# Keeping four w1 chunks and two query chunks in four slots of the gather ring, in a two-layer decoder trunk on one Trainium2 core

## The chip, the core and the metric

The kernel runs on one core of one Trainium2 chip. The metric is the time on the device in microseconds, from the start of the program to its end; the median of several runs counts, and lower is better. A difference of 0.2% (3.2 us here) is about the smallest that this measurement can tell from no change.

## What is computed

A trunk of two layers over 256 tokens of width 1024, in float32. Layer 0 mixes sparse attention with retention, layer 1 is a gated convolution module, and each is followed by a PEER step, in which every token picks 128 rows (8 heads, 16 picks each) out of 16384 experts and needs their `u` and `v` rows in full:

```python
q = (xf @ w_q).reshape(T, P_HEADS, 2, P_QDIM // 2)
...
eidx = (e1 * P_NKEYS + e2).reshape(T, P_HEADS * P_TOPK)
...
hb = jnp.einsum('td,tkd->tk', xb, u[ib])
act = jax.nn.gelu(hb, approximate=False) * gb
return jnp.einsum('tk,tkd->td', act, v[ib])
...
a = h @ w_pw1 + b_pw1                      # conformer module of layer 1
a = a[..., :D] * jax.nn.sigmoid(a[..., D:])
```

## The kernel before

The tokens are two tiles of 128, one token to a partition. The PEER work is four passes `p`: layer 0 tile 0, layer 0 tile 1, layer 1 tile 0, layer 1 tile 1. A pass has 8 rounds `i` of 16 picks, so there are 512 picks, numbered here n = 128p + 16i + r. One pick is one indirect gather by POOL (L441) of 8 KB for each of 128 partitions (`u` and `v` of one expert for each token), 1.05 MB, into one slot of `ring`, which has 16 slots. DVE takes the dot product of the `u` half with the token (L984), ACT turns four dots into gelu times gate and four diagonal matrices (L596 to L605), and PE multiplies those with the `v` half into PSUM (L1430), pick by pick in pairs, and counts each on the semaphore `v_multiplied`. A slot is free when its pick is multiplied. `AHEAD = 5` is the number of gathers that may be under way: gather n waits until gather n-5 has landed.

Everything else stands between these picks, in an order written out by hand. DVE has its top-k of the next queries (`heads_step`), the 31 taps of the convolution (`conv_taps`), norms and sums between dots, at fixed rounds and picks. PE has after each batch of four picks what `first_beside`, `beside` and `conv_beside` say: the query products (L1181 into `side`), the products with `w1` (`conv_in`, L1181 into `pm`) and `w2` (`conv_out`), and the scores (L1402). The convolution of tile 0 runs in pass 1, that of tile 1 in pass 2; `conv_in` stands at the (round, batch) pairs `CONV_INS = [(0, 2), (0, 3), (1, 1), (1, 2), (1, 3), (2, 0), (2, 1), (2, 2)]`. The queries of heads 6 and 7 of passes 2 and 3 are multiplied in round 1 of these passes, after batch 0.

The weights come in chunks of 1 MB through a buffer of two, `wbuf`, in the order of `CHUNKS`, issued by SP (L352); a chunk is loaded when PE has multiplied the one two places before it. The 8 chunks of `w1` are loaded once for each tile; query chunks 6 and 7 of layer 1 are loaded once for pass 2 and once for pass 3. Gathers and weights run on the same 16 DMA engines.

Of the kernel before, what the change touches and what calls it, by code (L numbers as in the profile page):

```python
# [7 lines left out]
D = 1024  # L8
KD = D // P
# [9 lines left out]
P_HEADS, P_TOP = 8, 16  # L19
# [16 lines left out]
RING = 16  # L36
# [20 lines left out]
X_OF_NORM = [0, 0, 1, 2, 3, 4, 5, 6, 7, 8]  # L57

def weight_chunks():

    order = [("o", 0, c) for c in range(4)] + [("q", 0, h) for h in range(4)]
    order += [("o", 1, c) for c in range(4)] + [("q", 0, h) for h in range(4, 8)] + [("q", 1, h) for h in range(4)]
    for p in (1, 2):
        order += [("w1", p - 1, c) for c in range(2)]
        if p == 2:
            order += [("q", 2, 6), ("q", 2, 7)]
        order += [("w1", p - 1, c) for c in range(2, KD)] + [("w2", p - 1, c) for c in range(4)]
        order += [("q", p + 1, h) for h in range(6)]
    return order + [("q", 3, 6), ("q", 3, 7)]


CHUNKS = weight_chunks()
SELECTIONS = [(0, 0), (0, 1), (0, 2), (1, 2), (0, 3), (1, 3), (1, 0), (1, 1)] + [(p, i) for p in (2, 3) for i in range(4)]


# [15 lines left out]
def hybrid_decoder_trunk_kernel(nc, x, gains, w_in, kv_norm, uk_t, uv_w, w_o, rot, decay,  # L91
# [9 lines left out]
    with ctx:  # L101
# [159 lines left out]
        lead_ready, gate_exp = sem("lead_ready"), sem("gate_exp")  # L261
        gathered = [sem(f"gathered{r}") for r in range(RING)]
        idx_copied, may_gather = sem("idx_copied"), sem("may_gather")
        picks_ready = [sem(f"picks_ready{t}") for t in range(TILES)]
# [44 lines left out]
        def _(sp):  # L309
# [24 lines left out]
            def multiplied(n):  # L334
# [6 lines left out]
                return (wo_ps if kind == "o" else w2_ps), p * 4 + c + 1  # L341

            def load_chunks(kind, p, first, end):

                view = {"o": w_o, "q": wq_l[p // 2], "w1": w1, "w2": w2}[kind]
                for c in range(first, end):
                    n = CHUNKS.index((kind, p, c))
                    if n >= WBUF:
                        sp.wait_ge(*multiplied(n - WBUF))
                    else:  # L350
                        sp.wait_ge(ret_s_ready, 1)
                    sp.dma_start(wbuf[:, n % WBUF, :, :].rearrange("p k c -> p (k c)"), view[:, c, :]) \  # L352
                      .then_inc(w_loaded[n % WBUF], 16)
# [12 lines left out]
            load_gain("bias", 0)  # L366
            load_chunks("w1", 0, 0, KD)
            load_gain("norm", 5)
# [20 lines left out]
        def _(pool):  # L389
# [23 lines left out]

            def gathers(p, first, pairs):

                layer, t = p // 2, p % 2
                rounds = PICKS // RING
                with pool.Fori(0, pairs) as i:
                    for half in range(2):
                        r0 = p * rounds + first + half  # L420
                        if p != 1:
                            pool.wait_ge(picks_ready[t], i * 2 + (layer * rounds + half + 1))
                        pool.wait_ge(v_multiplied, i * (2 * RING) + (r0 * RING + 1))
                        pool.sem_inc(may_gather, 1)
                        pool.tensor_copy(idx_now[:, half, :], eidx[:, t, ds(i * (2 * RING) + (first + half) * RING, RING)]) \  # L425
                            .then_inc(idx_copied, 1)
                        pool.wait_ge(idx_copied, i * 2 + (r0 + 1))
                        for r in range(RING):
                            freed = r0 * RING + r + 1
                            pool.wait_ge(v_multiplied, i * (2 * RING) + freed)  # L430
                            if r0 == 0 and r in in_use:
                                if in_use[r]:
                                    pool.wait_ge(proj_ps, job_of(*in_use[r]) + 1)
                                else:
                                    pool.wait_ge(b_t_ready, 2)
                            if r >= AHEAD:
                                pool.wait_ge(gathered[r - AHEAD], i * 32 + 16 * (r0 + 1))
                            elif p or half:
                                pool.wait_ge(gathered[r - AHEAD + RING], i * 32 + 16 * r0)
                            pool.sem_inc(may_gather, 1)  # L440
                            pool.indirect_dma_start(ring[:, r, :], None, table[layer],  # L441
                                                    bass.IndirectOffsetOnAxis(idx_now[:, half, r:r + 1], 0)) \
                                .then_inc(gathered[r], 16)

            pool.wait_ge(a_ready, 2)
            gathers(0, 0, 4)
            pool.wait_ge(picks_ready[1], P_HEADS - 2)
            gathers(1, 0, 1)
            pool.wait_ge(picks_ready[1], P_HEADS)
            gathers(1, 2, 3)  # L450
            gathers(2, 0, 4)
            gathers(3, 0, 4)

# [263 lines left out]
        def _(dve):  # L717
# [256 lines left out]
            def expert_round(p, i, between=None):  # L974


                t = p % 2
                rounds = PICKS // RING

                for r in range(RING):  # L980
                    if between:
                        between(r)
                    dve.wait_ge(gathered[r], i * 16 + 16 * (p * rounds + 1))
                    dve.scalar_tensor_tensor(out=ring[:, r, 0:D], in0=ring[:, r, 0:D], scalar=1.0, in1=h_tok[:, t, :],  # L984
                                             op0=ALU.mult, op1=ALU.mult, accum_out=hb[:, r:r + 1]).then_inc(dots_ready, 1)
# [183 lines left out]
        def _(pe):  # L1169
# [245 lines left out]
            def expert_round(p, i, between=None):  # L1415
# [4 lines left out]
                for b, (first, end) in enumerate(batches(p, i)):  # L1420
                    for r0 in range(first, end, 2):
                        pair = range(r0, min(r0 + 2, end))
                        pe.wait_ge(diag_ready, p * PICKS + i * RING + pair[-1] + 1)
                        for c in range(2):
                            for r in pair:
                                odd = r % 2 if (p, i) != LAST or r < RING - 1 else 0
                                for half in range(2):
                                    rows = slice(half * HALF, (half + 1) * HALF)
                                    j = (half + odd) % 2
                                    step = pe.matmul(acc[odd][c][j * HALF:(j + 1) * HALF, :], diag[rows, r % (2 * BATCH), :],  # L1430
                                                     ring[rows, r, D + c * COLS:D + (c + 1) * COLS],
                                                     start=(i == 0 and r0 == 0), stop=(i == 7 and r == last_pick[odd]))
# [172 lines left out]
```

## Time and profile before

| | |
|---|---|
| median of 3 runs | 1593.21 us (1592.16 to 1594.64) |
| the profiled execution | 1591.96 us, span of its instructions 1590.2 us |
| mean granted TensorE clock | 0.819 |
| busy over the span | PE 1020.0 us, DVE 1096.9 us, ACT 462.7 us, POOL 678.4 us |
| moved by DMA | 622.17 MB, mean 391 GB/s |

Busy time is a sum over stages with different limits, so it says little by itself: what matters is what each engine waits for in a stretch. The span falls into the mixer of layer 0 (to some 137 us, where the first gather is issued), pass 0, pass 1 (picks 128 to 255), pass 2 (256 to 383) and pass 3 (384 to 511).

### The profile page before, as it was taken

The page shows a single profiled execution, that of the slowest core. Times are in us where ns is not written, and L with a number is a line of the kernel's source. Part 1 is how long each engine was busy: PE and PEld are TensorE (multiplying, and loading weights), DVE is VectorE, ACT ScalarE, POOL GpSimd, SP SyncE. Part 2 cuts the span into 40 slices and gives each one's busy share as a digit, 9 for nine tenths or more (in the row PEclk, how much of TensorE's full clock was granted, in tenths as well). Part 3 has the DMA queues.
Part 4 walks back from the last instruction along what each step waited for, and adds up shares of the span by engine and source line. Part 5 has one row for each costly group of instructions (what it writes and reads, how often), then busy time and mean ns, then how long its engine had stood idle before and what let it go on. Part 6 is the DMA issues. An engine that isn't in the chain of part 4 may idle for free.

```text
span 1590.2 us, 20959 instructions
## 1 busy us (share of the span) xinstructions
PE 1020.0 (64%) x6998; PEld 536.9 (34%) x6998; DVE 1096.9 (69%) x2839; ACT 462.7 (29%) x1442; POOL 678.4 (43%) x566
## 2 busy tenths in 40 slices
PE   7999747555566586566745667546675557555565
PEld 7796424222333143223413335312332223111111
DVE  2745565887777877985457789899558777744445
ACT  2221313322223433333313333324142223322223
POOL 0002434443444445674334345465333435554552
PEclk9999878677777897878878879967987778787768
DMA  9046999999999999999999999999999999999996
GB/s 381 25 167 256 368 421 420 419 421 402 407 420 421 399 422 420 421 420 421 421 421 421 420 420 416 419 385 414 421 421 420 421 415 412 418 421 420 416 421 275
DMA packets 86883, 622.17 MB, mean 391 GB/s; under 512 B 9600, under 2 KB 10368, under 8 KB 12800
## 3 DMA queue, kind: packets, MB, share of 16 engines
q0 software_dynamic: 73728, 536.90, 81.7%
q1 hardware_dynamic: 12912, 83.74, 13.0%
q8 instruction: 55, 0.90, 0.2%
q14 instruction: 44, 0.36, 0.1%
q10 hardware_dynamic: 144, 0.26, 0.0%
HBM read 619.82 MB, written 1.05 MB: 390 GB/s over the span
## 4 chain that ended last, share of the span: by engine, by line
DMA 62%; PE 22%; DVE 11%; ACT 2%; issue 1%; DVEq 1%; ACTq 0%; POOL 0%; POOLq 0%
DMA ring<-experts_dram,idx_now 61%; PE side L1430 7%; PE pm L1181 7%; DVE ring L984 5%; PE side L1181 4%; ACT act_v L599 1%; DMA wbuf<-w_dram 1%; ACT diag_all L605 1%; DVE top_i L904 1%; DVE top_i L920 0%; DVE onehot L905 0%; PE side L1402 0%; DVE best_i L929 0%; DVE diag_all L932 0%; DVE best_i L940 0%
## 5 line engine op out<-in xcount | busy, mean ns | idle before, releaser
L441 POOL DMA_INDIRECT ring<-experts_dram,idx_now x512 | 659.4, 1288 | 734.4 <-DMA ring<-experts_dram,idx_now 398.2
L1430 PE MATMUL side<-ring,diag_all 64*64 64x512 f32 x2056 | 627.3, 766 | 537.6 <-ACT diag_all L605 537.6
L984 DVE SCALAR_TENSOR_TENSOR ring<-ring,h_tok 128x1024 f32<-128x1024 f32 x512 | 607.5, 1222 | 158.4 <-DMA ring<-experts_dram,idx_now 151.8
L1430 PE MATMUL pm<-ring,diag_all 64*64 64x512 f32 x2040 | 623.2, 766 | 0.0
L1430 PEld LDWEIGHTS side<-ring,diag_all 64*64 64x64 f32 x2056 | 172.7, 173 | 938.2 <-ACT diag_all L605 575.0
L596 ACT ACTIVATE ge<-hb 128x4 f32<-128x4 f32 (+1 forms) x130 | 26.7, 206 | 864.5 <-DVE ring L984 864.3
L1430 PEld LDWEIGHTS pm<-ring,diag_all 64*64 64x64 f32 x2040 | 170.6, 173 | 0.0
L605 ACT ACTIVATE diag_all<-ident,act_v 128x64 f32<-128x64 f32 x512 | 136.6, 336 | 10.6
L1053 DVE SCALAR_TENSOR_TENSOR conv_buf<-conv_buf,chan_sb 128x128 f32<-128x128 f32 x480 | 128.6, 340 | 0.0
L599 ACT ACTIVATE act_v<-ge,gates 128x1 f32<-128x1 f32 x512 | 109.2, 283 | 9.5 <-issue 0.7
L901 DVE MAX8 top_v<-side 128x8 f32<-128x128 f32 x64 | 15.2, 289 | 116.7 <-PE side L1402 116.6
L1181 PEld LDWEIGHTS side<-h_t,wbuf 128*128 128x128 f32 x768 | 87.0, 192 | 10.1 <-issue 9.4
L1181 PE MATMUL side<-h_t,wbuf 128*128 128x128 f32 x768 | 89.4, 277 | 0.5 <-DMA wbuf<-wq_dram 0.5
L1181 PEld LDWEIGHTS pm<-hc_t,wbuf 128*128 128x128 f32 x512 | 58.4, 192 | 13.4 <-issue 11.7
L1181 PE MATMUL pm<-hc_t,wbuf 128*128 128x128 f32 x512 | 61.3, 278 | 0.9 <-DMA wbuf<-w_dram 0.9
L425 POOL COPY idx_now<-eidx 128x16 uint32 (+1 forms) x32 | 12.4, 388 | 99.9 <-ACT conv_buf L547 73.3
L1181 PE MATMUL pm<-conv_buf,ring 128*128 128x128 f32 x448 | 53.7, 280 | 0.2 <-DVE ring L831 0.2
L596 ACT ACT_TABLE_LOAD x41 | 52.6, 1283 | 1.6
L1181 PEld LDWEIGHTS pm<-conv_buf,ring 128*128 128x128 f32 x448 | 52.3, 194 | 1.4 <-DVE ring L831 0.6
L984 DVE DVE_READ_ACCUMULATOR ring<-ring,h_tok 128x1 f32 x512 | 41.3, 81 | 0.0
L1181 PE MATMUL pm<-ring,conv_buf 128*128 128x512 f32 (+2 forms) x128 | 35.3, 429 | 1.1 <-ACT conv_buf L469 1.1
L1181 PE MATMUL pm<-wbuf,hc_t 128*128 128x256 f32 x128 | 30.6, 398 | 6.3 <-DMA wbuf<-w_dram 6.3
(200 smaller groups left out, 830.7 us busy)
## 6 DMA issues: line engine op xcount, KB each, us to landing
wbuf<-wq_dram SPq DMA_DIRECT2D x28, 1024.0 KB, 11.0
wbuf<-w_dram SPq DMA_DIRECT2D x24, 1024.0 KB, 9.8
ring<-w_in_dram SPq DMA_DIRECT2D x5, 2048.0 KB, 22.2
wbuf<-w_o_dram SPq DMA_DIRECT2D x8, 1024.0 KB, 7.9
ring<-experts_dram,idx_now POOLq DMA_INDIRECT x512, 11.7
gain<-gains_dram SPq DMA_DIRECT2D x7, 512.0 KB, 13.0
ring<-w_in_dram SPq DMA_DIRECT2D x1, 1696.0 KB, 9.7
x_tok<-x_dram SPq DMA_DIRECT2D x2, 512.0 KB, 4.8
```

The lines of the kernel that those rows point to most:

```text
L425: pool.tensor_copy(idx_now[:, half, :], eidx[:, t, ds(i * (2 * RING) + (first + half) * RING, RING)]) \
L441: pool.indirect_dma_start(ring[:, r, :], None, table[layer], bass.IndirectOffsetOnAxis(idx_now[:, half, r:r + 1], 0)) \
L596: act.activation(ge[:, first:end], hb[:, first:end], ACT.Gelu)
L599: last = act.activation(act_v[:, r:r + 1], ge[:, r:r + 1], ACT.Copy, scale=gates[:, t, i * RING + r:i * RING + r + 1])
L605: act.activation(diag[:, r % (2 * BATCH), :], ident2[:, :], ACT.Copy, scale=act_v[:, r:r + 1]).then_inc(diag_ready, 1)
L901: dve.max(top_v[:, b, j, 0:8], side[b, j])
L904: dve.max_index(top_i[:, b, j, 0:8], top_v[:, b, j, 0:8], side[b, j])
L984: dve.scalar_tensor_tensor(out=ring[:, r, 0:D], in0=ring[:, r, 0:D], scalar=1.0, in1=h_tok[:, t, :], op0=ALU.mult, op1=ALU.mult, accum_out ...
L1053: step = dve.scalar_tensor_tensor(out=dst, in0=src, scalar=tap, in1=dst, op0=ALU.mult, op1=ALU.add)
L1181: last = pe.matmul(dst, lhs(k), rhs(k), start=(k == 0), stop=(k == KD - 1))
L1430: step = pe.matmul(acc[odd][c][j * HALF:(j + 1) * HALF, :], diag[rows, r % (2 * BATCH), :], ring[rows, r, D + c * COLS:D + (c + 1) * COLS] ...
```

## The change

Ring slots 12 to 15 hold weights for a time. When tile 0's last picks of layer 0 (124 to 127) are multiplied, chunks 0 to 3 of `w1` are loaded into these four slots, and both tiles' convolutions read them there. When tile 1's `conv_in` is through with chunks 0 and 1, query chunks 6 and 7 of layer 1 go into slots 12 and 13 and serve passes 2 and 3. In all, six loads of 1 MB fall away. Slots 14 and 15 are given back to the gathers at pick 296, slots 12 and 13 at pick 416. So the gathers have 12 slots for picks 128 to 295, 14 for 296 to 415, and 16 otherwise. A pick takes the free slot that was used longest ago, by a table `SLOTS` made when the program is built; POOL's gathers, in loops with a register before, are written out one by one.

```diff
+KEPT = 4
+KEPT_IN = {("w1", c): RING - KEPT + c for c in range(KEPT)} | {("q", 6): RING - KEPT, ("q", 7): RING - KEPT + 1}
+KEPT_FROM = PICKS
+KEPT_TO = {RING - KEPT + c: 3 * PICKS + 2 * RING if c < 2 else 2 * PICKS + 2 * RING + 8 for c in range(KEPT)}
...
+def pick_slots():
+    last, uses, slots = {r: r - RING for r in range(RING)}, {r: 0 for r in range(RING)}, []
+    for n in range(4 * PICKS):
+        free = [r for r in range(RING) if r not in KEPT_TO or not KEPT_FROM <= n < KEPT_TO[r]]
+        r = min(free, key=lambda r: last[r])
+        uses[r] += 1
+        slots.append((r, uses[r], max(last[r], n - RING)))
+        last[r] = n
+    return slots
...
+            def load_kept(kind, p, c):
+                r = KEPT_IN[(kind, c)]
+                if kind == "w1":
+                    sp.wait_ge(v_multiplied, RING + max(n for n in range(KEPT_FROM) if SLOTS[n][0] == r) + 1)
+                else:
+                    sp.wait_ge(pw_ps, KD + r - RING + KEPT + 1)
+                view = {"q": wq_l[p // 2], "w1": w1}[kind]
+                sp.dma_start(ring[:, r, :], view[:, c, :]).then_inc(kept_loaded[r - RING + KEPT], 16)
...
-            load_chunks("w1", 0, 0, KD)
+            for c in range(KEPT):
+                load_kept("w1", 0, c)
+            load_chunks("w1", 0, KEPT, KD)
...
-            load_chunks("w1", 1, 0, 2)
-            load_chunks("q", 2, 6, 8)
-            load_chunks("w1", 1, 2, KD)
+            for c in (6, 7):
+                load_kept("q", 2, c)
+            load_chunks("w1", 1, KEPT, KD)
...
-            load_chunks("q", 3, 2, 8)
+            load_chunks("q", 3, 2, 6)
...
+                    for n in range(n0, n0 + RING):
+                        r, use, freed = SLOTS[n]
+                        if freed >= 0:
+                            pool.wait_ge(v_multiplied, RING + freed + 1)
...
+                        if n >= AHEAD:
+                            pool.wait_ge(gathered[SLOTS[n - AHEAD][0]], 16 * SLOTS[n - AHEAD][1])
                         pool.sem_inc(may_gather, 1)
+                        pool.indirect_dma_start(ring[:, r, :], None, table[layer],
+                                                bass.IndirectOffsetOnAxis(idx_now[:, i % 2, n - n0:n - n0 + 1], 0)) \
+                            .then_inc(gathered[r], 16)
...
             def chunk(kind, p, c):
+                if (kind, c) in KEPT_IN and (kind == "w1" or p > 1):
+                    r = KEPT_IN[(kind, c)]
+                    pe.wait_ge(kept_loaded[r - RING + KEPT], 32 if kind == "q" else 16)
+                    return ring[:, r, :].rearrange("p (k c) -> p k c", k=KD)
```

SP's queue around the start of pass 1, before the change: the bias row and the eight `w1` chunks of tile 0, two at a time through `wbuf` (line 332 loads a row of gains or biases, line 352 a weight chunk; the wait named is the semaphore of what must be multiplied first):

```order
L332 DMA gain<-b_dram 128x1024 [waits h_ready]
L352 DMA wbuf<-w_dram 128x2048 [waits q_ps] x2
L352 DMA wbuf<-w_dram 128x2048 [waits pw_ps] x6
L332 DMA gain<-gains_dram 128x1024 [waits h_ready]
L352 DMA wbuf<-w_dram 128x2048 [waits pw_ps] x2
```

The same place after the change (line 351 loads a row, 370 a chunk into the ring, 381 a chunk into `wbuf`):

```order
L351 DMA gain<-b_dram 128x1024 [waits h_ready]
L370 DMA ring<-w_dram 128x2048 [waits v_multiplied] x4
L381 DMA wbuf<-w_dram 128x2048 [waits q_ps] x2
L381 DMA wbuf<-w_dram 128x2048 [waits pw_ps] x2
L351 DMA gain<-gains_dram 128x1024 [waits h_ready]
L381 DMA wbuf<-w_dram 128x2048 [waits pw_ps] x2
L381 DMA wbuf<-w_dram 128x2048 [waits w2_ps] x2
```

Four chunks now wait for multiplied picks, and chunks 4 and 5 stand right behind them in one queue, with a wait that is long over.

POOL's queue at the boundary between rounds 0 and 1 of pass 1, picks 142 to 147, before the change (the copy sets the indices of the next round; `gatheredN` is the landing of the gather into slot N, here that of pick n-5):

```order
L441 DMA ring<-experts_dram,idx_now 128x2048 [waits v_multiplied,gathered9]
L441 DMA ring<-experts_dram,idx_now 128x2048 [waits v_multiplied,gathered10]
L425 COPY idx_now<-eidx 128x16 [waits v_multiplied]
L441 DMA ring<-experts_dram,idx_now 128x2048 [waits gathered11,idx_copied,v_multiplied]
L441 DMA ring<-experts_dram,idx_now 128x2048 [waits v_multiplied,gathered12]
L441 DMA ring<-experts_dram,idx_now 128x2048 [waits v_multiplied,gathered13]
L441 DMA ring<-experts_dram,idx_now 128x2048 [waits v_multiplied,gathered14]
```

The same seven places after the change:

```order
L472 DMA ring<-experts_dram,idx_now 128x2048 [waits v_multiplied,gathered9]
L472 DMA ring<-experts_dram,idx_now 128x2048 [waits v_multiplied,gathered10]
L455 COPY idx_now<-eidx 128x16 [waits v_multiplied]
L472 DMA ring<-experts_dram,idx_now 128x2048 [waits gathered11,idx_copied,v_multiplied]
L472 DMA ring<-experts_dram,idx_now 128x2048 [waits v_multiplied,gathered0]
L472 DMA ring<-experts_dram,idx_now 128x2048 [waits v_multiplied,gathered1]
L472 DMA ring<-experts_dram,idx_now 128x2048 [waits v_multiplied,gathered2]
```

After slot 11 comes slot 0, and 12 to 15 are left out. The order of gathers, dots and products is the same; what moved is the slot that each uses, and with it the multiplied pick that POOL waits for: from pick 140 on n-12, in place of n-16.

## Rows read from the trace of the kernel before

**Rows 1.** Page, part 2: DMA share and rate in 40 slices.

```profile
DMA  9046999999999999999999999999999999999996
GB/s 381 25 167 256 368 421 420 419 421 402 407 420 421 399 422 420 421 420 421 421 421 421 420 420 416 419 385 414 421 421 420 421 415 412 418 421 420 416 421 275
```

**Rows 2.** Page, parts 3 and 6: queues; issues (count, KB, us to landing).

```profile
q0 software_dynamic: 73728, 536.90, 81.7%
q1 hardware_dynamic: 12912, 83.74, 13.0%
...
wbuf<-w_dram SPq DMA_DIRECT2D x24, 1024.0 KB, 9.8
...
ring<-experts_dram,idx_now POOLq DMA_INDIRECT x512, 11.7
```

**Rows 3.** Windows: PE, PEld, DVE, ACT, POOL busy; clock, DMA share, GB/s.

```profile
490.00:810.00 320.00, 201.10 (x1406) 100.44 (x1409) 233.86 (x583) 107.17 (x318) 163.86 (x118) 0.83 1.01 418
810.00:1331.00 521.00, 319.75 (x2231) 161.63 (x2224) 404.81 (x1127) 161.92 (x498) 235.65 (x192) 0.81 1.01 416
1331.00:1580.00 249.00, 148.52 (x911) 47.50 (x912) 137.51 (x269) 58.92 (x241) 120.42 (x101) 0.77 0.99 412
```

**Rows 4.** DVE's waits for gathers in 490:810, 810:1331, 1331:1580 (us, times, longest).

```profile
DVE ring L984 <- DMA ring<-experts_dram,idx_now: 31.3, 23, 3.7
...
DVE ring L984 <- DMA ring<-experts_dram,idx_now: 8.2, 7, 1.6
...
DVE ring L984 <- DMA ring<-experts_dram,idx_now: 108.6, 87, 2.2
```

**Rows 5.** Timeline around 1180: DVE's last gather wait, its next wait; PE.

```profile
1183.16 1.22 DVE L984 SCALAR_TENSOR_TENSOR ring<-ring,h_tok 128x1024 f32<-128x1024 f32 x1 [1.23 <-DMA ring<-experts_dram,idx_now]
...
1193.52 0.94 DVE L901 MAX8 top_v<-side 128x8 f32<-128x128 f32 x4 [9.12 <-PE side L1402]
...
1178.29 7.41 PE L1181 MATMUL side<-h_t,wbuf 128*128 128x128 f32 x64
```

**Rows 6.** The gathers' line: time from issue to landing, min, median, max.

```profile
DMA to landing us min/median/max: 5.7/11.7/20.3
```

**Rows 7.** Timeline of SP: issues of weight chunks that fall away or move.

```profile
490.24 3.90 SPq L352 DMA_DIRECT2D wbuf<-w_dram  x2
...
896.08 3.90 SPq L352 DMA_DIRECT2D wbuf<-w_dram  x2
...
1271.77 3.90 SPq L352 DMA_DIRECT2D wbuf<-wq_dram  x2
```

**Rows 8.** Pass 1: PE ends 128; POOL's 140, copy, 144; DVE's dot 147.

```profile
541.27 1.06 PE L1430 MATMUL pm<-ring,diag_all 64*64 64x512 f32 x2
...
529.94 0.94 POOL L441 DMA_INDIRECT ring<-experts_dram,idx_now  x1 [2.94 <-DMA ring<-experts_dram,idx_now]
...
542.50 0.78 POOL L425 COPY idx_now<-eidx 128x16 uint32<-128x16 uint32 x1 [5.02 <-PE pm L1430]
544.11 1.09 POOL L441 DMA_INDIRECT ring<-experts_dram,idx_now  x1 [0.83 <-PE pm L1430]
...
564.25 1.22 DVE L984 SCALAR_TENSOR_TENSOR ring<-ring,h_tok 128x1024 f32<-128x1024 f32 x1
...
569.49 0.35 DVE L1038 SCALAR_TENSOR_TENSOR conv_buf<-pm,chan_sb,gate_sig 128x128 f32<-128x128 f32 x1 [2.87 <-ACT gate_sig L616]
```

**Rows 9.** Before pick 200: PE finishing 184, 185; DVE's dot 200.

```profile
694.00 1.06 PE L1430 MATMUL pm<-ring,diag_all 64*64 64x512 f32 x2
...
713.01 1.22 DVE L984 SCALAR_TENSOR_TENSOR ring<-ring,h_tok 128x1024 f32<-128x1024 f32 x1 [0.42 <-DMA ring<-experts_dram,idx_now]
```

**Rows 10.** Pick 412: PE ends 396; POOL's gather 410; DVE's dot 412.

```profile
1317.99 1.06 PE L1430 MATMUL pm<-ring,diag_all 64*64 64x512 f32 x2
...
1314.68 1.89 POOL L441 DMA_INDIRECT ring<-experts_dram,idx_now  x1 [1.70 <-issue]
...
1331.60 1.22 DVE L984 SCALAR_TENSOR_TENSOR ring<-ring,h_tok 128x1024 f32<-128x1024 f32 x1 [0.19 <-DMA ring<-experts_dram,idx_now]
```

More of the change, by code:

```diff
@@ L262, in hybrid_decoder_trunk_kernel @@
         gathered = [sem(f"gathered{r}") for r in range(RING)]
+        kept_loaded = [sem(f"kept_loaded{c}") for c in range(KEPT)]
         idx_copied, may_gather = sem("idx_copied"), sem("may_gather")
@@ L412, in _, with gathers @@
                                        base=P * t, pattern=[[-1, s]], channel_multiplier=1).then_inc(done, 1)
-            def gathers(p, first, pairs):
+            def gathers(p, first, end):
                 layer, t = p // 2, p % 2
[L417 to L423, printed above, removed]
-                        pool.sem_inc(may_gather, 1)
[L425 to L443, printed above, removed]
@@ new lines, in gathers @@
+                for i in range(first, end):
+                    n0 = p * PICKS + i * RING
+                    if p != 1:
+                        pool.wait_ge(picks_ready[t], layer * P_HEADS + i + 1)
+                    if n0:
+                        pool.wait_ge(v_multiplied, n0 + 1)
+                    pool.sem_inc(may_gather, 1)
+                    pool.tensor_copy(idx_now[:, i % 2, :], eidx[:, t, i * RING:(i + 1) * RING]).then_inc(idx_copied, 1)
+                    pool.wait_ge(idx_copied, n0 // RING + 1)
+                    for n in range(n0, n0 + RING):
+                        r, use, freed = SLOTS[n]
+                        if freed >= 0:
+                            pool.wait_ge(v_multiplied, RING + freed + 1)
+                        if n < RING and r in in_use:
+                            if in_use[r]:
+                                pool.wait_ge(proj_ps, job_of(*in_use[r]) + 1)
+                            else:
+                                pool.wait_ge(b_t_ready, 2)
+                        if r >= RING - KEPT and n >= KEPT_TO[r] and all(SLOTS[m][0] != r for m in range(KEPT_TO[r], n)):
+                            c = r - RING + KEPT
+                            pool.wait_ge(*((q_ps, nth_head(3, 3, c)) if c < 2 else (pw_ps, KD + c + 1)))
+                        if n >= AHEAD:
+                            pool.wait_ge(gathered[SLOTS[n - AHEAD][0]], 16 * SLOTS[n - AHEAD][1])
+                        pool.sem_inc(may_gather, 1)
+                        pool.indirect_dma_start(ring[:, r, :], None, table[layer],
+                                                bass.IndirectOffsetOnAxis(idx_now[:, i % 2, n - n0:n - n0 + 1], 0)) \
+                            .then_inc(gathered[r], 16)
@@ L445, in _ @@
             pool.wait_ge(a_ready, 2)
[L446 removed]
+            gathers(0, 0, 8)
             pool.wait_ge(picks_ready[1], P_HEADS - 2)
[L448 removed]
+            gathers(1, 0, 2)
             pool.wait_ge(picks_ready[1], P_HEADS)
[L450 to L452 removed]
+            gathers(1, 2, 8)
+            gathers(2, 0, 8)
+            gathers(3, 0, 8)
         @block.scalar
@@ L982, in expert_round @@
                         between(r)
-                    dve.wait_ge(gathered[r], i * 16 + 16 * (p * rounds + 1))
-                    dve.scalar_tensor_tensor(out=ring[:, r, 0:D], in0=ring[:, r, 0:D], scalar=1.0, in1=h_tok[:, t, :],
+                    slot, use, _ = SLOTS[p * PICKS + i * RING + r]
+                    dve.wait_ge(gathered[slot], 16 * use)
+                    dve.scalar_tensor_tensor(out=ring[:, slot, 0:D], in0=ring[:, slot, 0:D], scalar=1.0, in1=h_tok[:, t, :],
                                              op0=ALU.mult, op1=ALU.mult, accum_out=hb[:, r:r + 1]).then_inc(dots_ready, 1)
```

12 lines of the change are left out of this document (5 added, 7 removed).

## The prediction

> **What bounds the kernel now.** I number picks n = 128p + 16i + r. I first read the rate of the DMA engines: from slice 6 on it stands at 400 to 421 GB/s with few dips, also in the windows 490 to 810 us and 810 to 1331 us, where it moves 418 and 416 GB/s [rows 1, 3]. The gathers are 81.7% of the engines' span and SP's weights 13.0% [rows 2]. By that view the kernel is bound by transfers, and each byte less is time gained. The second view says otherwise for one stretch: how long DVE, the first user of each gather, waited for gathers. From 490 to 810 us it waited 31.3 us in 23 waits, from 1331 us to the end 108.6 us in 87, which is every pick; but from 810 to 1331 us only 8.2 us in 7 waits [rows 4]. In these 521 us (picks 233 to 411) DVE works off top-k steps, convolution taps and dots at its own pace, and the transfers run ahead of it into the ring. Of the 8.2 us, six waits lie between 1170 and 1184 us, and the timeline shows that they hide behind PE: right after the last of them (1.23 us) DVE waits 9.12 us for scores from PE, which had to do query products from 1178.29 to 1185.70 us before it came to these picks at all [rows 5]. So the kernel has three parts: transfers set the pace to pick 232, the chain DVE, ACT, PE from there to pick 411, and transfers again from 412 to the end.
>
> **What the fewer bytes give.** Six chunks of 1024 KB are 6.29 MB, at 421 GB/s [rows 1] 14.9 us of the DMA engines. Four of them stood at 896 us and after, two at 1271 us [rows 7]. Both places lie in the middle part, where DVE does not wait for gathers. The gathers then run further ahead, until they find no free slot; dot 411 ends where it did. What can be gained is what the transfers may be ahead of DVE when the third part begins, and the slots limit that.
>
> **Where the third part starts.** A gather needs, after the product that frees its slot, 0.83 us to its issue (the gather behind the index copy [rows 8]) and then at least 5.7 us to land, the least of all 512, with the queue nearly empty; the median is 11.7, with others ahead of it [rows 6]. With 14 slots gather 410 waits for the product of pick 396, the first behind a long DVE step. It ends at 1317.99 + 1.06 = 1319.05 us [rows 10]. Landing is 1319.05 + 0.83 + 5.7 = 1325.6 us, and pick 412, two gathers of 2.49 us later (1.049 MB at 421 GB/s), lands at 1330.6 us. Before, DVE began dot 412 on its landing, at 1331.60 us [rows 10]. So at the best 1.0 us of the 14.9 is left. (With 16 slots pick 412 itself would wait for pick 396, and 6.0 us would be left.) Between 5.7 and 11.7 us I take 7.2, near the short end, since the ring is drained then: +1.5 us. This term: -1.0 + 1.5 = +0.5 us.
>
> A rule of the Trainium skill gives another price (DMA: Bandwidth & Descriptors, Anatomy of one DMA): some 2.0 us fixed and the bytes at 436 GB/s. That is 4.4 us for a gather, an estimate from the page; the trace's least is 5.7 us. By the page the best case would be 2.3 us in place of 1.0.
>
> **What the slots cost at pass 1.** The four kept chunks wait for picks 124 to 127. Gather 140 waited for pick 124 too, before, and was issued at 529.94 us [rows 8], so they start about then, and chunks 4 and 5 follow at once: 6.29 MB, 14.9 us of all engines, to 545 us. Before, the first two were issued at 490.24 us [rows 7]. Gather 140 now needs slot 0 and so pick 128, multiplied at 541.27 + 1.06 = 542.33 us [rows 8]. It lands at 542.33 + 0.83 + 5.7 = 548.9 us, up to 1.5 us later where the loads still take half of the engines. Pick 147, seven gathers of 2.49 us on, lands at 566.3 to 567.8 us. DVE began its dot at 564.25 us [rows 8], so DVE is 2.1 to 3.6 us late; I take 3. The next wait of DVE, 2.87 us for the gate's sigmoid [rows 8], comes from ACT's work on these same dots, and moves with them. It does not absorb the delay.
>
> DVE catches up with the gathers at pick 200, which it started on landing at 713.01 us [rows 9]. With 12 slots gather 196 waits for pick 184, 694.00 + 1.06 = 695.06 us, 3 us later now: 698.1 + 0.83 + 5.7 = 704.6, and pick 200 lands at 714.6 us, 1.6 us later than before; with the 7.2 us of above, 3.1. I take 2.5. From 200 to 232 DVE mostly waits for gathers, so this passes whole to pick 232, and from there by the chain to pick 411 and to the third part, whose start was worked out from the product of pick 396.
>
> **Costs taken as nothing.** SP: the kept chunks hold the queue to 530 us; chunk 0 is needed behind the products of picks 136 to 139, and even 128's ends at 542.33 us. Without that cover PE would stand, and the gates and taps behind it. SP's waits for query chunks 6 and 7 are the ones of before, and only `w1` chunks 4 and 5 queue behind them. POOL's register steps go, 0.05 us or so a gather, and five gathers under way cover it. Pass 0 keeps its 16 slots. In pass 2 gathers come later by up to some 10 us, but there the ring lies well ahead of DVE, which waited for almost none [rows 4]. From nothing to a few us is possible here, and only as loss.
>
> **Sum.** +2.5 for the chain, +0.5 for the restart: +3.0 us on the profiled execution's 1591.96 us (span 1590.2 and 1.8 around it) is 1595.0 us. The median of the runs is 1.25 us above that execution: 1593.21 + 3.0 = **1596.2 us**, 0.19% slower, at the edge of what can be told from no change (0.2%, 3.2 us).
>
> **Rivals.** *The bytes count.* The Trainium skill says (DMA: Bandwidth & Descriptors, Issuing engines are not separate DMA queues) that transfers of all issuing engines share the same 16 DMA engines; so fewer weights would be faster gathers. The rates in rows 1 and 3 speak for it: the engines stand at 416 GB/s in the middle part too. Against it speak DVE's waits there. As a mechanism: if the gathers of the middle part let DVE and PE finish sooner, or if the engines lose less at restarts than I think, up to 14.9 us come off: 1593.2 - 14.9 = 1578.3; half, 1585.8. It decides for itself if dot 411 ends before 1326 us. I give 1578 to 1590 a chance of 0.18.
>
> *The restarts cost more.* Each time the ring is full and then drains, a landing may take the 11.7 us of the median, not 5.7 to 7.2, as gathers free in pairs and weights land beside them. Then pick 200 is 1.6 + 6.0 = 7.6 us late, and pick 412 4.5 us more than I took: 1593.2 + 7.6 - 1.0 + 6.0 = 1605.8 us. It decides from some 9 us from issue to landing. Chance 0.26, 1600 to 1606.
>
> *Mine*, 1591 to 1600: 0.56. Slots that do not bind (the change would do only what it says, and the gain would still not arrive) give 1592 and are its low end.
>
> **Numbers.** The range of 8 in 10 cuts the far half of the bytes' case and little of the other: 1586 to 1606; mine alone is 1591 to 1600. Faster by over 0.2%: 0.17, nearly all of the bytes' case. Slower by over 0.2% (above 1596.4): the second rival's 0.26 and 0.19 of mine, 0.45. Within: 0.38.
>
> **What would show it.** SP's queue at 77.4 MB. Dips under 400 GB/s at 540 to 560 us and several between 860 and 1330 us, where now there is hardly one. POOL's waits for the product line longer. Dot 200 begins at 714 to 717 us, and dot 412 2 to 5 us later than now; the 99 picks behind it take 2.5 us each as before. In the middle DVE's waits for gathers stay under 15 us. I am wrong if dot 147 is on time (the loads and gather 140 then did not collide), if the middle part gets shorter, or if gathers after a full ring land 9 us or more after issue.

## The result, and the profile after

The changed kernel takes 1598.84 us (median of 6 runs, 1596.89 to 1600.9), the kernel before 1592.79 us beside it (6 runs, 1592.16 to 1594.64). The ratio is 1.0032, 95% interval 1.0022 to 1.0043: slower by 3.5 to 6.8 us. The profiled execution of after took 1596.89 us, span 1595.2, granted clock 0.817; it is the shortest of its six, so its trace tells a little less of the loss than the medians.

The page's part 2 of after, in slices of some 40 us, as in [rows 1]:

```profile
DMA  9046999999999999999999989999999999999997
GB/s 382 18 172 237 372 421 421 421 421 407 401 420 421 398 422 421 403 369 422 421 421 396 421 325 421 420 422 412 417 405 421 421 374 394 421 421 421 421 421 304
```

Parts 3 and 6 of the page, the queues and the gathers, as in [rows 2]:

```profile
q0 software_dynamic: 73728, 536.90, 81.7%
q1 hardware_dynamic: 12048, 77.45, 12.1%
...
ring<-experts_dram,idx_now POOLq DMA_INDIRECT x512, 11.6
```

The six loads are gone (83.74 to 77.45 MB), and there are dips that were not there: 369 in the slice from some 678 us, 396 in the one from some 837 us, 325 from some 917 us, 374 and 394 from some 1276 us. The windows, with the columns of [rows 3]:

```profile
490.00:810.00 320.00, 207.73 (x1418) 102.03 (x1416) 233.92 (x583) 106.56 (x314) 158.44 (x116) 0.81 1.00 410
810.00:1331.00 521.00, 315.08 (x2192) 159.46 (x2196) 400.90 (x1121) 161.97 (x497) 240.25 (x190) 0.80 0.98 404
1331.00:1580.00 249.00, 148.50 (x920) 48.25 (x916) 141.54 (x275) 58.94 (x242) 125.60 (x105) 0.78 1.01 421
```

In the middle part 12 GB/s less are moved over 521 us, 6.3 MB: the saved bytes. DVE did not get more done there for it (400.90 us busy, 404.81 before). DVE's waits for gathers in the same three windows (us, times, longest), for [rows 4]:

```profile
DVE ring L1015 <- DMA ring<-experts_dram,idx_now: 37.3, 29, 2.8
...
DVE ring L1015 <- DMA ring<-experts_dram,idx_now: 14.8, 7, 3.7
...
DVE ring L1015 <- DMA ring<-experts_dram,idx_now: 105.9, 85, 1.4
```

Pass 1, for [rows 8], in the timeline of after: PE ends the product of pick 128; POOL issues gather 140; DVE starts the dots of picks 140, 141 and 147, each on a landing:

```profile
544.21 1.06 PE L1466 MATMUL pm<-ring,diag_all 64*64 64x512 f32 x2
...
546.10 0.94 POOL L472 DMA_INDIRECT ring<-experts_dram,idx_now  x1 [20.87 <-PE pm L1466]
...
553.23 1.23 DVE L1015 SCALAR_TENSOR_TENSOR ring<-ring,h_tok 128x1024 f32<-128x1024 f32 x1 [1.02 <-DMA ring<-experts_dram,idx_now]
555.78 1.22 DVE L1015 SCALAR_TENSOR_TENSOR ring<-ring,h_tok 128x1024 f32<-128x1024 f32 x1 [1.31 <-DMA ring<-experts_dram,idx_now]
...
572.21 1.23 DVE L1015 SCALAR_TENSOR_TENSOR ring<-ring,h_tok 128x1024 f32<-128x1024 f32 x1 [1.25 <-DMA ring<-experts_dram,idx_now]
```

POOL stands 20.87 us before gather 140. Dot 147 begins 572.21 - 564.25 = 8.0 us later than before. Further on, POOL's gather 196, DVE's dot 200, for [rows 9]:

```profile
703.74 1.51 POOL L472 DMA_INDIRECT ring<-experts_dram,idx_now  x1 [5.61 <-PE pm L1466]
...
721.19 1.22 DVE L1015 SCALAR_TENSOR_TENSOR ring<-ring,h_tok 128x1024 f32<-128x1024 f32 x1 [0.46 <-DMA ring<-experts_dram,idx_now]
```

Dot 200 is 8.2 us later. And the start of the third part, for [rows 10]: PE ends product 396; POOL issues gather 410; DVE starts dots 412 and 413:

```profile
1324.21 1.06 PE L1466 MATMUL pm<-ring,diag_all 64*64 64x512 f32 x2
...
1326.11 0.94 POOL L472 DMA_INDIRECT ring<-experts_dram,idx_now  x1 [6.90 <-PE pm L1466]
...
1337.70 1.23 DVE L1015 SCALAR_TENSOR_TENSOR ring<-ring,h_tok 128x1024 f32<-128x1024 f32 x1
1340.19 1.23 DVE L1015 SCALAR_TENSOR_TENSOR ring<-ring,h_tok 128x1024 f32<-128x1024 f32 x1 [1.26 <-DMA ring<-experts_dram,idx_now]
```

Gather 410 waits for 396 as foreseen, and dot 412 begins 1337.70 - 1331.60 = 6.1 us later. The whole line of gathers has, from issue to landing (for [rows 6]):

```profile
DMA to landing us min/median/max: 5.4/11.6/20.7
```

The wait of POOL's gathers for products grew from 86.5 us (50 waits, the longest 6.8) to 211.8 us (71 waits, the longest 20.9):

```profile
POOL ring L472 <- PE pm L1466: 211.8, 71, 20.9
```

### The profile page after: what moved, and what is told of

It is laid out like the page before. It is cut to its first block, busy times and chain, and to the rows that moved or that the text cites. A ratio compares the mean times of both kernels' runs of the same rounds, so it can differ in the third digit from the quotient of the medians.

```text
span 1595.2 us, 20346 instructions
## 1 busy us (share of the span) xinstructions
PE 1026.8 (64%) x6998; PEld 538.7 (34%) x6998; DVE 1097.8 (69%) x2839; ACT 463.1 (29%) x1442; POOL 683.1 (43%) x566
## 3 DMA queue, kind: packets, MB, share of 16 engines
q1 hardware_dynamic: 12048, 77.45, 12.1%
## 4 chain that ended last, share of the span: by engine, by line
DVE 36%; PE 29%; DMA 21%; ACT 7%; issue 3%; DVEq 2%; ACTq 1%; POOL 0%; POOLq 0%
DMA ring<-experts_dram,idx_now 20%; DVE ring L1015 15%; PE side L1466 12%; DVE conv_buf L1084 8%; PE pm L1212 7%; PE side L1212 6%; ACT diag_all L636 2%; ACT act_v L630 2%; DVE top_i L935 1%; DVE top_i L951 1%; DVE onehot L936 1%; ACT L647 1%; DVE diag_all L963 1%; DVE best_i L960 1%; DVE best_i L971 1%
## 5 line engine op out<-in xcount | busy, mean ns | idle before, releaser
L472 POOL DMA_INDIRECT ring<-experts_dram,idx_now x512 | 667.3, 1303 | 740.1 <-DMA ring<-experts_dram,idx_now 362.8
L1466 PE MATMUL side<-ring,diag_all 64*64 64x512 f32 x2056 | 634.0, 773 | 536.5 <-ACT diag_all L636 536.4
L1466 PE MATMUL pm<-ring,diag_all 64*64 64x512 f32 x2040 | 629.9, 774 | 0.0
L1212 PEld LDWEIGHTS side<-h_t,wbuf 128*128 128x128 f32 x640 | 72.5, 192 | 8.1 <-issue 8.1
L1212 PE MATMUL side<-h_t,wbuf 128*128 128x128 f32 x640 | 74.3, 276 | 0.0
L455 POOL COPY idx_now<-eidx 128x16 uint32<-128x16 uint32 x32 | 9.2, 288 | 92.5 <-ACT conv_buf L578 72.9
L1212 PEld LDWEIGHTS pm<-hc_t,wbuf 128*128 128x128 f32 x256 | 29.2, 192 | 6.8 <-issue 6.8
L1212 PEld LDWEIGHTS pm<-hc_t,ring 128*128 128x128 f32 x256 | 29.2, 192 | 5.7 <-issue 5.7
```

Source lines behind the costliest of these rows:

```text
L472: pool.indirect_dma_start(ring[:, r, :], None, table[layer], bass.IndirectOffsetOnAxis(idx_now[:, i % 2, n - n0:n - n0 + 1], 0)) \
L1212: last = pe.matmul(dst, lhs(k), rhs(k), start=(k == 0), stop=(k == KD - 1))
```

## The experiments

The table gives, for each kernel, the median, the ratio to the kernel before with its interval, and from its trace how much later than in the trace of before the dots of some picks ended (us, less is earlier). Picks 120 and before are the same work in all, so the column for 120 is the spread from one execution to another, and 147 is read against it. Each kernel has one trace, so a difference of a us or so between two rows can be such spread too.

| kernel | median us | ratio | 120 | 147 | 232 | 396 | 412 | 511 |
|---|---|---|---|---|---|---|---|---|
| after | 1598.84 | 1.0032 [1.0022, 1.0043] | 1.7 | 8.0 | 8.4 | 6.2 | 6.1 | 4.9 |
| e_unroll | 1593.33 | 0.9999 [0.999, 1.0007] | 1.5 | 1.4 | 2.6 | 2.9 | 2.8 | 1.4 |
| e_bytes | 1588.97 | 0.9974 [0.9959, 0.9988] | 3.3 | 3.3 | 2.8 | 1.5 | 1.3 | -3.5 |
| e_slots | 1605.46 | 1.0076 [1.0063, 1.0089] | 1.0 | 7.0 | 11.3 | 12.9 | 13.3 | 13.1 |
| e_two | 1589.69 | 0.9974 [0.9963, 0.9984] | 0.8 | 0.8 | 2.0 | 1.8 | 1.6 | -3.1 |
| e_late | 1599.33 | 1.0044 [1.0027, 1.0061] | 0.7 | 6.3 | 9.5 | 5.7 | 5.6 | 5.1 |
| e_two_q | 1595.51 | 1.0002 [0.9988, 1.0016] | -0.1 | -0.1 | 2.2 | 3.3 | 3.6 | 3.5 |
| e_pass1 | 1603.12 | 1.0056 [1.0043, 1.0069] | 2.8 | 7.8 | 12.4 | 10.8 | 11.0 | 11.1 |
| e_rest | 1597.96 | 1.0024 [1.0011, 1.0037] | 2.0 | 2.1 | 5.0 | 3.6 | 6.2 | 6.1 |
| e_back | 1594.09 | 0.9999 [0.999, 1.0008] | 1.9 | 6.9 | 8.0 | 5.5 | 5.3 | 3.6 |
| e_three | 1589.34 | 0.9984 [0.9967, 1.0] | 2.7 | 6.1 | 4.4 | 0.9 | 0.8 | -2.9 |

The kernel before stood at 1593.29 us in the first four (26 runs), 1594.26 us in the second four (18), 1593.92 us in the last two (22). Three parts of the change are mixed: POOL's loop written out, slots taken from the gathers, loads left out. The first four kernels take them apart.

The diffs are against the changed kernel, but for e_bytes, which is against e_unroll, and show the lines that decide. Where a load is not saved, it stands in `CHUNKS` and in SP's queue where it stood before the change.

**e_unroll: nothing kept, 16 slots, POOL's gathers written out.**

```diff
-KEPT = 4
-KEPT_IN = {("w1", c): RING - KEPT + c for c in range(KEPT)} | {("q", 6): RING - KEPT, ("q", 7): RING - KEPT + 1}
+KEPT = 0
+KEPT_IN = {}
...
```

> The changed kernel with nothing kept: 16 slots for the gathers all the time, all 60 chunks through wbuf as before. All that is left of the change is POOL's gathers written out one by one without register steps. If the cost of the change lies in the slots, this is the kernel before: 1592.8 us, within 2 us. If the written-out gathers cost something by themselves (the changed kernel is 1.7 us late at pick 120 already, before any slot is held), it is 1594.5 us or more, and late at pick 120.

1593.33 us, ratio 0.9999 [0.999, 1.0007]. Writing the loop out costs and brings nothing that can be told. The lateness of 1.5 us at pick 120 in this trace is not seen in the median, so it is the execution's.

**e_bytes: as e_unroll, and the six loads left out.** The products that used these chunks read another array that lies in SBUF; the engines' work is the same.

```diff
-            load_chunks("w1", 1, 0, 2)
-            load_chunks("w1", 1, 2, KD)
+            load_chunks("w1", 1, 4, KD)
-            load_chunks("q", 3, 2, 8)
+            load_chunks("q", 3, 2, 6)
```

> The six loads taken away, and no slot held: 16 slots all the time, w1 chunks 0 to 3 of tile 1 and query chunks 6 and 7 of pass 3 are not loaded, and their products read the small table of keys in their place, with the same number of matmuls (so the output isn't the reference's). If the middle part is set by DVE and PE and the ring's slots limit how far the gathers run ahead, pick 412 can land 6.0 us earlier at most: 1586.8 us, down to 1592 if the restart is slow. If the bytes count, the whole 14.9 us come off: 1577.9 us.

1588.97 us, 0.9974: 4.1 us come off, of 14.9 us of transfers. DVE's waits for gathers in the middle part fall to 3.7 us, but that passes on in little: against pick 120 dot 360 is 6.5 us earlier (-3.2 and 3.3), and by dot 396 this is 1.8 us (1.5). DVE's wait for scores from PE that follows dot 360, 9.12 us before ([rows 5]), is 15.28 us here and takes it up. The larger part of the gain comes behind pick 412, from 1.3 to -3.5 us: gather 412 waits for product 396, lands at 1326.90 us and lies ready 5.97 us before its dot begins at 1332.87 us, the 6.0 us that the prediction had given for 16 slots. The waits row and the window 810 to 1331 us of this kernel:

```profile
DVE ring L1017 <- DMA ring<-experts_dram,idx_now: 3.7, 2, 2.5
```

```profile
810.00:1331.00 521.00, 320.54 (x2231) 162.17 (x2232) 403.91 (x1125) 163.92 (x505) 254.44 (x193) 0.81 1.00 407
```

**e_slots: the slots held as in the change, all chunks loaded through `wbuf` as before.**

```diff
-KEPT_IN = {("w1", c): RING - KEPT + c for c in range(KEPT)} | {("q", 6): RING - KEPT, ("q", 7): RING - KEPT + 1}
+KEPT_IN = {}
...
```

> The slots held as in the changed kernel (12 for picks 128 to 295, 14 to 415), but nothing kept in them: all chunks go through wbuf as before. If the held slots are what costs, the delays at picks 140, 196 and 410 of the changed kernel are all there, and the six loads are added: 1599 to 1606 us. If the cost of the changed kernel is the burst of six chunks at 530 us, this one has none and stands at 1593 to 1595 us, with dot 147 on time.

1605.46 us, 1.0076: the slots alone cost 12.1 us. Six loads fewer bring the change back to 1.0032, that is by 0.44% or 7.0 us.

**e_two: two `w1` chunks kept, in slots 14 and 15, given back at picks 282 and 286; no query chunk.** Two loads saved, 14 slots for picks 128 to 281.

```diff
-KEPT = 4
+KEPT = 2
...
+KEPT_IN = {("w1", c): RING - KEPT + c for c in range(2)}
...
-KEPT_TO = {RING - KEPT + c: 3 * PICKS + 2 * RING if c < 2 else 2 * PICKS + 2 * RING + 8 for c in range(KEPT)}
+KEPT_TO = {RING - KEPT + c: 2 * PICKS + 2 * RING - 6 + 4 * c for c in range(KEPT)}
```

> Two w1 chunks kept in slots 14 and 15, given back at picks 282 and 286 when tile 1 has used them, no query chunk kept: 14 slots for picks 128 to 281, 16 in pass 3, two loads less. By my sum with 14 slots gather 142 waits for pick 128 and lands at some 549 us, before DVE wants it, and gather 196 waits for pick 182, 11 us earlier than 184: no delay in pass 1. With 16 slots pick 412 is the first bound by pick 396. So up to 5.0 us (two loads) come off: 1588 to 1591 us. If any held slot costs, 1594 us or more.

1589.69 us, 0.9974: faster than both kernels, and as fast as e_bytes, which saves six loads and keeps 16 slots. Dot 147 is on time. The cap is seen in the timeline of e_two: POOL's gather 412 is issued at 1321.70 us, when product 396 is done. It lands at 1327.54 us, 5.66 us before DVE begins its dot, and that lead is what the third part gains (4.7 us in this trace).

```profile
1321.70 0.94 POOL L474 DMA_INDIRECT ring<-experts_dram,idx_now  x1 [6.90 <-PE pm L1468]
```

**e_late: the change, but `w1` chunks 4 and 5 of tile 0 are held back, so four loads and not six fall together at 530 us.**

```diff
+                    if (kind, p) == ("w1", 0) and c in (4, 5):
+                        sp.wait_ge(pw_ps, c - 3)
```

> The changed kernel, but the w1 chunks 4 and 5 of tile 0 are held back on SP until conv_in 0 and 1 are multiplied, so that four loads, not six, land in one burst around 530 to 545 us beside gather 140. What the slots cost at pass 1 (12 slots make gather 140 wait for product 128): gather 140 lands at most 1.5 us sooner, dot 147 stays 6 to 8 us later than before the change, median 1597 to 1599. Rival, the burst: six loads at once are what delays products 128 to 139 and gather 140; then dot 147 is under 3 us late and the median is 1593 to 1595.

1599.33 us, 1.0044, as the change. Gather 140 lands 5.6 us after its issue, in place of 7.1, but dot 147 is no better (6.3 - 0.7 = 5.6 us late; in the change 8.0 - 1.7 = 6.3). The timeline of e_late, dot 147:

```profile
570.50 1.23 DVE L1017 SCALAR_TENSOR_TENSOR ring<-ring,h_tok 128x1024 f32<-128x1024 f32 x1 [3.46 <-DMA ring<-experts_dram,idx_now]
```

The burst is not what makes dot 147 late; the rival falls. The median lies 0.3 us above the range I had expected. But dot 232 is 9.5 - 0.7 = 8.8 us late here and 8.4 - 1.7 = 6.7 in the change: the two loads held back come beside gathers later.

**e_two_q: slots 14 and 15 keep two `w1` chunks, then query chunks 6 and 7 to pick 415.** Four loads saved.

```diff
-KEPT = 4
+KEPT = 2
-KEPT_IN = {("w1", c): RING - KEPT + c for c in range(KEPT)} | {("q", 6): RING - KEPT, ("q", 7): RING - KEPT + 1}
+KEPT_IN = {("w1", c): RING - KEPT + c for c in range(2)} | {("q", 6): RING - KEPT, ("q", 7): RING - KEPT + 1}
```

> Two slots (14 and 15) held from pick 128 to 415: w1 chunks 0 and 1, then query chunks 6 and 7; four loads fall away. By the slots: 14 in pass 1 cost nothing there (dot 147 and pick 232 within 2 us of before), but pick 410 waits for the product of 396, so pick 412 lands about where it did: -1 to +1, median 1592 to 1594, in place of the 1589.7 of the kernel that saves two loads and has 16 slots there. Rival, the bytes count: twice the bytes saved of that kernel, 9.9 us less than before, 1583 to 1587.

1595.51 us (1589.26 to 1598.4), 1.0002 [0.9988, 1.0016]; the median lies above the 1592 to 1594 I had expected. It saves twice the bytes of e_two and loses its whole gain, because gather 410, not 412, waits for 396, and dot 412 begins on the landing of its gather, without a lead: holding the slots to 416 costs what they save.

**e_pass1 and e_rest: nothing kept, all loads as before; slots 12 to 15 left out for picks 128 to 255 only, or in the change's pattern from 256 on only.**

```diff
 e_pass1
+KEPT_IN = {}
+KEPT_TO = {RING - KEPT + c: 2 * PICKS for c in range(KEPT)}
...
 e_rest
+KEPT_IN = {}
-KEPT_FROM = PICKS
+KEPT_FROM = 2 * PICKS
```

> Nothing is kept, all weights go through wbuf as before; slots 12 to 15 are only left out for picks 128 to 255, and are free again from 256. By the slots in pass 1: dot 147 is 6 to 8 us late, pick 232 8 to 11 us, and since transfers are never ahead in the middle part here, the end is as late as that: 1601 to 1604. Rival, the later stretches with 12 and 14 slots carry half of the loss: under 5 us, 1594 to 1598.

> Nothing is kept, all weights go through wbuf as before; the gathers have 16 slots to pick 255, 12 for picks 256 to 295, 14 for 296 to 415, 16 from 416. By the slots in pass 1: nothing is late up to 256; in the middle part transfers are not ahead, so the wait of 410 for 396 costs 0 to 2 us: 1593 to 1596. Rival, the later stretches carry half of the loss: 5 us or more, 1598 to 1600.

e_pass1: 1603.12 us, 1.0056, 8.9 us. e_rest: 1597.96 us, 1.0024, 3.8 us, between what the two theories had said; it loses 2.6 us between dots 396 and 412, where transfers that are not ahead meet the wait for 396. Together 12.7 us, and e_slots, which has both, measured 12.1. In e_pass1 gather 140 is issued as late as in the change, and dot 147 begins at the same time (against pick 120 it is 5.0 us late, in the change 6.3); but no load fills the gap. POOL's gather 140 and DVE's dot 147:

```profile
545.95 0.94 POOL L472 DMA_INDIRECT ring<-experts_dram,idx_now  x1 [16.13 <-PE pm L1466]
...
572.03 1.23 DVE L1015 SCALAR_TENSOR_TENSOR ring<-ring,h_tok 128x1024 f32<-128x1024 f32 x1 [2.80 <-DMA ring<-experts_dram,idx_now]
```

The window 540 to 550 us of e_pass1, then of the change (last two columns: DMA share, GB/s):

```profile
540.00:550.00 10.00, 6.32 (x40) 2.06 (x44) 8.33 (x16) 7.72 (x22) 3.44 (x3) 0.75 0.25 79
```

```profile
540.00:550.00 10.00, 7.28 (x40) 2.35 (x44) 8.33 (x16) 7.85 (x22) 3.30 (x3) 0.63 0.99 394
```

**e_back: four `w1` chunks kept as in the change, all four slots given back at pick 296, no query chunk kept.** Four loads saved.

```diff
+KEPT_IN = {("w1", c): RING - KEPT + c for c in range(4)}
...
+KEPT_TO = {RING - KEPT + c: 2 * PICKS + 2 * RING + 8 for c in range(KEPT)}
```

> Four w1 chunks kept from pick 128 as in the change, but all four slots are given back at pick 296 and no query chunk is kept: four loads of 1 MB saved, not six, and 16 slots where pick 412 is reached. By the slots: pass 1 costs the same as in the change (dot 147 6 to 8 us late), but pick 412 is no longer behind the wait of 410 for 396 and lands 4 to 6 us sooner against dot 396 than in the change; median 1593 to 1595. Rival, the bytes count: two loads more than the change, 0 to +5 us against it, 1599 to 1604.

1594.09 us, 0.9999: two loads more than the change, and about 5 us less by the ratios, so the rival of the bytes falls. The reason I had given holds in part only. In the profiled execution of e_back the landing of pick 412 gains 1.8 us against dot 396, not 4 to 6. Gather 412 does wait for product 396, which ends at 1323.47 + 1.06 = 1324.53 us; it is issued 0.83 us later. The view puts POOL's wait down to a landing, but 407, the landing it needs, had come at 1322.52 us. With four loads saved the gathers were not far enough ahead for the stop to drain the engines: 410 and 411 were still under way and landed at 1329.94 and 1332.41 us, so 412 landed 9.8 us after its issue and not 5.5, at 1335.14 us, 1.8 us before its dot.

```profile
1323.47 1.06 PE L1468 MATMUL pm<-ring,diag_all 64*64 64x512 f32 x2
...
1325.36 0.94 POOL L474 DMA_INDIRECT ring<-experts_dram,idx_now  x1 [3.31 <-DMA ring<-experts_dram,idx_now]
```

The traces differ by 1.3 us at the last pick, the medians by 4.7; e_back's profiled execution was 1.7 us above its median and after's 2.0 below.

**e_three: three `w1` chunks kept, 13 slots from pick 128, given back from pick 282 to 290.**

```diff
-KEPT = 4
+KEPT = 3
+KEPT_IN = {("w1", c): RING - KEPT + c for c in range(3)}
...
+KEPT_TO = {RING - KEPT + c: 2 * PICKS + 2 * RING - 6 + 4 * c for c in range(KEPT)}
```

> Three w1 chunks kept in slots 13 to 15 from pick 128 to 286 to 294, 13 slots in between, 16 after; three loads saved. By the slots: gather 141 waits for the product of 128, one gather later than with 12 slots, so dot 147 is 2.5 us less late than in the change, 3 to 5 us; pick 412 is capped as with two chunks: median 1592 to 1594. Rival, the bytes count: one load more saved than with two chunks, -2.5 us: 1587 to 1588.

1589.34 us, ratio 0.9984 [0.9967, 1.0]. Dot 147 is 6.1 - 2.7 = 3.4 us late, between 0 with 14 slots and 5.0 to 6.3 with 12: a dose, some 2 to 3 us for each slot, about the 2.49 us of one gather. Gather 141 is the one that waits for product 128:

```profile
545.88 0.94 POOL L474 DMA_INDIRECT ring<-experts_dram,idx_now  x1 [12.29 <-PE pm L1468]
```

The median lies under the 1592 to 1594 I had expected, since the 3.4 us are gone by pick 396 (0.9 us against 2.7 at pick 120). The ratio says less than the median, 2.6 us and not 4.6; one of the 11 runs took 1601.18 us. By either it is no better than e_two, so the third load brings nothing that can be told.

## Why the prediction was right, and where it was off

The prediction was 1596.2 us, 3.0 us slower; measured are 1598.84 us, 5.1 us slower by the ratio and 6.0 by the medians. The direction held, and the mechanism in its main lines: the bytes do not pass on in the middle part, and the held slots cost more at pass 1 than they give back. The size came near in part by luck: the term of pass 1 was some 4 us too small, gains from the loads were left out, and some 2 us were given back at a place that the sum did not have.

**What bounds the kernel, and what the fewer bytes give.** That the saved bytes are not passed on in the middle part is shown by e_bytes: 14.9 us of transfers fall away, 4.1 us of time. Of what is left with 16 slots I had said 6.0 us, and the lead at pick 412 is 5.97 us in e_bytes. And two loads (e_two) give as much as six (e_bytes), which is the cap by product 396. What I did not have is that the loads are worth more where the slots are short: from e_slots to the change they bring 7.0 us. At pick 232 the change is 8.4 - 1.7 = 6.7 us late, e_slots 11.3 - 1.0 = 10.3; of this, the place of the loads is one part: in the change six loads fill the gap that the stopped gathers leave at 540 us (394 GB/s), while in e_pass1 the gap is nearly empty (79 GB/s), and the same bytes come beside gathers. The traces of the others with 12 slots there go the same way: 6.1 us late at pick 232 with all six loads in the gap (e_back), 8.8 with four (e_late), 9.6 with none (e_pass1). From pick 232 to 412 the change wins back 2.3 us, while e_slots loses 2.0 more. That is not a wait of DVE for gathers: these waits are 14.8 us in the change and 15.3 in e_slots. But PE's waits for weights in the window 810 to 1331 us are 7.3 us in e_slots and 3.4 in the change. The third `w1` chunk of tile 1 is one case: PE in e_slots, waiting for its landing, and DVE behind it; then PE in the change, which reads the chunk in the ring without a wait:

```profile
977.88 6.55 PE L1215 MATMUL pm<-hc_t,wbuf 128*128 128x128 f32 x32 [3.23 <-DMA wbuf<-w_dram]
...
984.87 0.35 DVE L1072 SCALAR_TENSOR_TENSOR conv_buf<-pm,chan_sb,gate_sig 128x128 f32<-128x128 f32 x1 [2.25 <-ACT gate_sig L650]
```

```profile
971.84 3.84 PE L1212 MATMUL pm<-hc_t,ring 128*128 128x128 f32 x32
```

Between dots 272 and 288 e_slots loses 2.4 us by it (9.8 to 12.2), the change nothing (7.1 and 7.1). So a load saved in the middle part can also be a wait of PE saved, which the prediction did not count. It is not always worth time: in e_unroll and e_pass1 PE waits 2.2 and 2.3 us for this chunk, and DVE does not wait behind it.

**What the slots cost at pass 1: the term that was mis-sized.** I had put it at 3 us at dot 147 and 2.5 us at dot 200, 232 and from there on. Against pick 120 it measured 6.3 us at dot 147, 6.5 us at 200, 6.7 us at 232, and in the five kernels with 12 slots there 5.0 to 6.3 us at 147. The steps, in the trace of after: product 128 ends at 545.27 us and not 542.33, 1.8 of it the run's own lag before any slot was held, 1.1 from a wait of DVE for PE's last products of pass 0; the issue follows 0.83 us behind, as I had said; the landing takes 7.1 us, my upper bound; then the seven gathers to pick 147 take 19.0 us and not the 17.4 of seven times 2.49. DVE's wait, which is not there before the change:

```profile
534.39 1.28 DVE L1021 TENSOR_TENSOR x_tok<-x_tok,side 128x512 f32<-128x512 f32 x2 [1.05 <-PE pm L1466]
```

From 530 to 535 us the granted clock is 0.63 here, 1.00 before and 0.95 in e_back, which is the same program all through pass 1 and has no such wait; so this 1.1 us is the execution's.

The interval of 2.49 us was the other wrong step: it holds where the gathers follow one another without a stop, not behind one. From the landing of 140 to that of 147 no weight packet moves in the change; the gathers' queue alone moves 7.96 MB, where seven gathers are 7.34 (queues in the window 553.21 to 572.18 us). The rest belongs to gathers behind 147, which run beside it. The four gathers from 196 to 200 take 11.4 us in place of 10.0, and 11.2 to 11.3 in the other four kernels with 12 slots; in the change no weight packet lies between them either (window 709.74 to 721.17 us, 4.70 MB where four gathers are 4.20):

```profile
q0 software_dynamic: 1097, 7.96, 100.6%
```

```profile
q0 software_dynamic: 638, 4.70, 99.5%
```

In e_slots, e_late and e_pass1 1.0 MB of weights lies between 140 and 147 too. From the issue of gather 140 to the landing of 147 I had reckoned 23.1 to 24.6 us. It is 26.0 to 27.0 us in the five kernels. And the delay was not absorbed at pick 200: gather 200 lands 0.46 us after DVE is ready for it. My arithmetic for pick 200 (gather 196, product 184) had the right path, from a start that was too small and with the same interval too short.

**Where the third part starts.** +0.5 us predicted from dot 396 to dot 412; measured -0.1 in the change (6.2 to 6.1), -0.1 in e_late, +0.3 in e_two_q. Gather 410 is issued 0.84 us after product 396 ends and lands 5.5 us later, where I had taken 7.2; but 412 lands 6.0 us behind it and not 5.0, so the two errors nearly cancel. Where no loads are saved the same slots cost 2.6 us there (e_rest), so it is right that the bytes saved here mostly pay for the slots held. That the queries' two slots to pick 416 are not worth it is shown by e_two_q against e_two: 0.9974 becomes 1.0002.

**Costs taken as nothing.** POOL's written-out loop: shown (e_unroll). In pass 2 I had allowed "a few us" as a loss; the later stretches with all loads cost 3.8 us (e_rest), 2.6 of it between dots 396 and 412.

**The middle part gave 2.3 us back, which I had at nothing.** Of this 1.9 us lie in one place: dot 232 is 8.4 us late, dot 236 6.5. Between them DVE waits for scores from PE, and those stand on the batch of picks 228 to 231, whose last dot is 7.7 us late, and on PE. From the start of that batch's products to the end of the scores PE takes 7.4 us before and 6.1 in the change, at a granted clock of 0.63 and 0.76. DVE's wait before, then in the change:

```profile
816.90 0.94 DVE L901 MAX8 top_v<-side 128x8 f32<-128x128 f32 x4 [6.31 <-PE side L1402]
```

```profile
823.35 0.94 DVE L932 MAX8 top_v<-side 128x8 f32<-128x128 f32 x4 [4.38 <-PE side L1437]
```

In the other ten traces PE takes 6.0 to 7.1 us there, less than in the trace of before in every one, also where nothing is held (e_unroll, 6.7). So 1.3 us of what was given back lies in the one trace that all rows of the table are read against.

The ledger, in the ratios: slots in pass 1 +8.9 us, slots from pass 2 on +3.8, six loads less -7.0, sum +5.7; the change is +5.1. Only one part of this is a test: that 8.9 and 3.8 add up to the 12.1 of e_slots; the -7.0 is itself the change less e_slots. My +2.5 and +0.5 had smaller terms of both signs: a slot cost of 12 us and a gain of 7 us from the loads were not in the sum.

**The signs.** SP's queue at 77.45 MB, the dips behind 860 us, POOL's longer waits for products and DVE's 14.8 us (under 15) in the middle came. The rate at 540 to 560 us did not dip (394 and 405 GB/s, where 346 and 409 had stood), since the loads filled the gap. Dot 200 at 721.19 us and dot 412 6.1 us later lie outside what I had given. I had written that I am wrong if the middle part gets shorter: it did, by the 2.3 us above, though not by saved bytes at dot 236, before which no load had fallen away.

Two readings of rows were off. The 0.83 us of [rows 8] is POOL's idle time behind the index copy, 1.78 us after product 128; that a gather follows its product by 0.83 us is shown by gathers 140 and 410 of the change. And from 1331 us on DVE waited 87 times in 100 picks, not at every pick.

**The rivals.** *The bytes count*: its upper case (1578) is excluded by e_bytes, which has all the bytes and none of the slots and reaches 1589. *The restarts cost more* had the right size for pass 1 (7.6 us late at pick 200; 8.2 measured, 6.5 of it the change's) by the wrong cause: gather 140 lands 5.4 to 8.6 us after its issue in the five kernels with 12 slots, not 11.7. At pick 412 it was wrong.

The Trainium skill (DMA: Bandwidth & Descriptors, Anatomy of one DMA) has by my estimate 4.4 us for one such gather. No gather of the 512 in the change landed in under 5.4 us; the measurement decides.

## What to carry to other kernels

A buffer that runs ahead of its consumer is worth what it covers: count, at each long step of the consumer, how many entries are used up while none comes free. Here 14 of 16 slots cover pass 1's, 13 and 12 each cost about one more transfer's time, and with 12 the loss passes to the end where no load is saved (e_pass1). Bytes saved while the transfers are ahead of the consumer buy mostly lead, and the slots cap the lead: with all or nearly all slots, two loads brought all that six did. A load that is saved can also spare the engine that uses it a wait. So take slots only for the stretch in which they pay, and give them back before the next place where the transfers become the bound.

## What was not expected of the hardware

After a stop an 8 KB by 128 gather lands 5.4 to 5.6 us after its issue if the engines are nearly empty (e_slots, e_late and e_pass1 at pick 140, the change at pick 410). The next ones do not follow at 2.5 us each from the start: the four behind gather 140 take 10.9 to 11.7 us in e_slots, e_late and e_pass1, and the four behind 196 and 410 11.0 to 11.4 in the change, with no weights between them, in place of 10.0. So a stop costs the gap and some 1 to 1.5 us more. A gap of 10 us in the gathers can be filled by weight loads at nearly the full rate (394 against 79 GB/s): loads that wait for just that moment are partly free.
